# A two-layer decoder trunk with expert lookup: one 8 KB gather per token for u and v, and all V rows summed on TensorE

## What is computed

```python
def _peer(h, w_q, sub_keys, u_tab, v_tab):
    ...
    def chunk(xc):
        q = (xc @ w_q).reshape(C, PEER_HEADS, 2, PEER_HALF)
        s = jnp.einsum('thpd,hpkd->thpk', q, sub_keys).astype(jnp.float32)
        sv, si = lax.top_k(s, PEER_TOPK)
        ...
        top, pos = lax.top_k(cand, PEER_TOPK)
        eidx = jnp.take_along_axis(cidx, pos, axis=-1)
        g = jax.nn.softmax(top, axis=-1)
        a = jnp.einsum('thkd,td->thk', u_tab[eidx], xc).astype(jnp.float32)
        w = (g * jax.nn.gelu(a)).astype(xc.dtype)
        return jnp.einsum('thk,thkd->td', w, v_tab[eidx])
```

## Time and profile before

| | us |
|---|---|
| median of 3 runs (lowest, highest) | 3302.86 (3289.01, 3326.77) |
| the profiled execution, its own time | 3275.28 |
| its span, first to last instruction | 3273.5 |
| first dot of a gathered row | 147.7 |

### The profile page before, as it was taken

How to read it: one execution, slowest core, us unless ns; L and a number is a source line. 1 busy time by engine, 2 the same in 40 slices (tenths; PEclk the granted TensorE clock), 3 DMA queues, 4 the chain that set the end, 5 groups by cost and what they waited for, 6 DMA issues and landing times. The chain is left out here.

```text
span 3273.5 us, 27575 instructions
## 1 busy us (share of the span) xinstructions
PE 2517.0 (77%) x7696; PEld 1421.7 (43%) x7696; DVE 2320.6 (71%) x5442; ACT 677.6 (21%) x1655; POOL 2313.0 (71%) x2052
## 2 busy tenths in 40 slices
PE   6569877987778779977787887987688777666667
PEld 5446444753444435633444444643354443222222
DVE  2495779668789985668569887577667888555554
ACT  2112212123312211123112122133411211100000
POOL 0256767666777777777778777777777777777776
PEclk9779988988888889988898888998899899877888
DMA  6499999998999999999999999999999999999999
GB/s 262 159 333 414 383 411 401 359 393 310 345 411 379 377 358 411 411 410 366 373 410 388 377 390 357 412 381 344 348 394 410 362 382 365 369 368 381 367 371 350
DMA packets 317239, 1210.29 MB, mean 370 GB/s; under 512 B 37280, under 2 KB 37536, under 8 KB 301728
## 3 DMA queue, kind: packets, MB, share of 16 engines
q0 software_dynamic: 294912, 1073.87, 85.4%
q1 hardware_dynamic: 22176, 134.66, 10.3%
HBM read 1206.29 MB, written 2.10 MB: 369 GB/s over the span
## 5 line engine op out<-in xcount | busy, mean ns | idle before, releaser
L832 PE MATMUL psY<-ring,diag 128*128 128x512 f32 x3120 | 1642.2, 671 | 469.2 <-DMA ring<-in_v,idx 203.2
L482 POOL DMA_INDIRECT ring<-in_u,idx x1024 | 1155.1, 1128 | 573.1 <-issue 293.6
L1094 DVE CUSTOM_DVE_ANT_0 ring<-ring,htok 128x1024 f32<-128x1024 f32 x1024 | 1232.7, 1223 | 373.6 <-DMA ring<-in_u,idx 326.8
L482 POOL DMA_INDIRECT ring<-in_v,idx x1024 | 1157.7, 1131 | 375.5 <-issue 303.9
L832 PEld LDWEIGHTS psY<-ring,diag 128*128 128x128 f32 x3120 | 638.0, 214 | 1265.3 <-issue 897.7
L1103 DVE SCALAR_TENSOR_TENSOR x<-ring,wgt,x 128x1024 f32<-128x1024 f32 x244 | 313.6, 1285 | 40.9 <-DMA ring<-in_v,idx 35.1
L704 PE MATMUL psP<-hT,wr 128*128 128x256 f32 (+1 forms) x1664 | 328.9, 354 | 11.3 <-issue 10.1
L708 PE MATMUL psP<-wr,hT 128*128 128x256 f32 x1344 | 313.2, 387 | 15.9 <-issue 8.6
L704 PEld LDWEIGHTS psP<-hT,wr 128*128 128x128 f32 x1664 | 285.7, 202 | 82.1 <-issue 55.5
L708 PEld LDWEIGHTS psP<-wr,hT 128*128 128x128 f32 x1344 | 261.1, 195 | 89.1 <-issue 43.7
L671 ACT ACTIVATE diag<-cst,wgt 128x128 f32<-128x128 f32 x780 | 252.7, 390 | 132.9 <-DVE wgt L1114 67.2
(11 more groups left out here) (125 smaller groups left out, 1660.3 us busy)
## 6 DMA issues: line engine op xcount, KB each, us to landing
wr<-in_w_in SPq DMA_DIRECT2D x44, 1024.0 KB
wr<-in_w_q SPq DMA_DIRECT2D x40, 1024.0 KB
ring<-in_u,idx POOLq DMA_INDIRECT x1024
ring<-in_v,idx POOLq DMA_INDIRECT x1024
wr<-in_w_out SPq DMA_DIRECT2D x16, 1024.0 KB
ring<-in_w_in SPq DMA_DIRECT2D x11, 1024.0 KB, 17.0
probs<-in_subkeys SPq DMA_DIRECT2D x5, 1024.0 KB
ring<-in_w_out SPq DMA_DIRECT2D x4, 1024.0 KB, 15.2
```

Source lines behind the costliest of these rows:

```text
L482: pool.indirect_dma_start(out=ring[:, q % NB], out_offset=None, in_=table, in_offset=bass.IndirectOffsetOnAxis(ap=idx[:, s % NS, n:n + 1], ...
L832: last = nc.tensor.matmul(psY[:, b * 512:(b + 1) * 512], diag[:, m % ND], r[:, b * 512:(b + 1) * 512], start=first, stop=final)
L1094: v.tensor_tensor_reduce(out=r, in0=r, in1=htok[:, s % NS], scale=1.0, scalar=0.0, op0=ALU.mult, op1=ALU.add, accum_out=adot[:, J % 2, k:k ...
```

## The change

The two tables of a layer are joined into one of 8 KB rows (u, then v) when inputs are prepared. POOL issues one gather a row, 1024 in place of 2048, into a ring of `NR` = 10 slots of 8 KB per partition (80 KB in place of 76). The slot is free when the row's v part has been summed. The lag of a head goes: DVE takes the dot of row q, ACT then makes Gelu, weight and diagonal for that row alone (`NG` = 1 row at a time), and writes the diagonal over the first 128 numbers of the row's u part; PE sums row q - 3 (`ROW_LAG`) from the slot. `vector_rows` is empty, so PE sums all 1024 rows. The product with the gate moves from DVE (once a head) to ACT (once a row). The buffers `diag` and the semaphore `a_gelu` go. The schedule of the other parts is not touched. The early pieces lie in ten slots in place of nine.

```diff
-NB = 19
+NR = 10
...
-ND = 12
-LEAD = 5
+NG = 1
+ROW_LAG = 3
...
 def vector_rows(J):
-    return BUSY_ROWS.get(J, (3, 7, 11, 15))
...
+    return ()
...
-        ring = sb("ring", [P, NB, D])
+        ring = sb("ring", [P, NR, 2 * D])
...
         def _(pool):
-            for q, (kind, J, k) in enumerate(plan):
...
+            for q in range(SLOTS * STEPS):
+                J, k = divmod(q, TOPK)
+                s, n = divmod(q, SLOTS)
+                if k == 0:
+                    pool.wait_ge(idx_ready, TOP_NO[s, J % PH] + 1)
                     if J == 0:
                         pool.wait_ge(piece_ready, W_EARLY)
-                if q >= NB:
-                    k0, J0, i0 = plan[q - NB]
-                    if k0 == "u":
-                        pool.wait_ge(dotted, TOPK * J0 + i0 + 1)
-                    else:
-                        by, m = V_NO[J0, i0]
-                        pool.wait_ge(vx_used if by else v_used, m + 1)
...
+                if q >= NR:
+                    by, m = V_NO[divmod(q - NR, TOPK)]
+                    pool.wait_ge(vx_used if by else v_used, m + 1)
+                pool.indirect_dma_start(out=ring[:, q % NR], out_offset=None, in_=tables[s // NC],
...
         def _(act):
...
+            for q in range(SLOTS * STEPS + 1):
+                if q and q % NG == 0:
+                    J, k = divmod(q - NG, TOPK)
+                    s, n = divmod(q - NG, SLOTS)
+                    act.wait_ge(dotted, q)
+                    link(nc.scalar.activation(gl[:, J % 2, k:k + NG], adot[:, J % 2, k:k + NG], ACT.Gelu_apprx_tanh))
+                    if k == 0:
+                        act.wait_ge(gate_ready, TOP_NO[s, J % PH] + 1)
+                    for i in range(NG):
+                        last = nc.scalar.activation(wgt[:, J % 2, k + i:k + i + 1], gate[:, s % NS, n + i:n + i + 1], ACT.Copy,
+                                                    scale=gl[:, J % 2, k + i:k + i + 1])
+                    last.then_inc(w_ready, 1)
+                    act.wait_ge(w_ready, q // NG)
+                    for i in range(NG):
+                        if V_NO[J, k + i][0] == 0:
+                            nc.scalar.activation(ring[:, (q - NG + i) % NR, 0:P], ident, ACT.Copy,
+                                                 scale=wgt[:, J % 2, k + i:k + i + 1]).then_inc(diag_ready, 1)
+                for part, s, i in at_slot("act", q):
+                    front(s, part, i)
...
         def _(pe):
...
+            for q in range(SLOTS * STEPS + ROW_LAG):
+                r = q - ROW_LAG
+                by, m = V_NO.get(divmod(r, TOPK), (1, 0))
+                if by == 0:
...
+                    landed(pe, r)
+                    pe.wait_ge(diag_ready, m + 1)
...
+                    for b in range(2):
+                        last = nc.tensor.matmul(psY[:, b * 512:(b + 1) * 512], ring[:, r % NR, 0:P],
+                                                ring[:, r % NR, D + b * 512:D + (b + 1) * 512], start=first, stop=final)
+                    last.then_inc(v_used, 1)
```

More of the change, by code:

```diff
@@ L211, in constants @@
     return c
[L214 to L223, removed]
 def trunk(nc, x_in, cst_in, w_in, w_out, w_q, subkeys, w_sgu, b_sgu, conv_w, g_mix, g_head, g_ffn,
           g_sgu, g_qd, g_kd, g_qs, g_ks, *rest):
-    tables_u, tables_v, out = rest[:DEPTH], rest[DEPTH:2 * DEPTH], rest[2 * DEPTH]
-    plan = gather_plan()
-    at = {g: q for q, g in enumerate(plan)}
+    tables, out = rest[:DEPTH], rest[DEPTH]
     with ExitStack() as ctx:
@@ L319, in trunk @@
         w_landed = [sem(f"w_landed{i}") for i in range(NW)]
-        we_landed = [sem(f"we_landed{i}") for i in range(NB // 2)]
-        g_landed = [sem(f"g_landed{i}") for i in range(NB)]
+        we_landed = [sem(f"we_landed{i}") for i in range(NR)]
+        g_landed = [sem(f"g_landed{i}") for i in range(NR)]
         piece_ready = sem("piece_ready")
@@ L819, in _ @@
                     front(s, part, i)
[L820 to L836, removed]
+            for q in range(SLOTS * STEPS + ROW_LAG):
+                r = q - ROW_LAG
+                by, m = V_NO.get(divmod(r, TOPK), (1, 0))
+                if by == 0:
+                    s = r // SLOTS
+                    first, final = m == v_rows(PH * s, 0), m == v_rows(PH * (s + 1), 0) - 1
+                    landed(pe, r)
+                    pe.wait_ge(diag_ready, m + 1)
+                    if first and s:
+                        pe.wait_ge(x_done, s)
+                    for b in range(2):
+                        last = nc.tensor.matmul(psY[:, b * 512:(b + 1) * 512], ring[:, r % NR, 0:P],
+                                                ring[:, r % NR, D + b * 512:D + (b + 1) * 512], start=first, stop=final)
+                    last.then_inc(v_used, 1)
+                for part, s, i in at_slot("pe", q):
+                    front(s, part, i)
         @block.vector
@@ L1087, in _ @@
                     front(s, part, i)
[L1088 to L1102, removed]
-                        v.scalar_tensor_tensor(out=xs, in0=ring[:, at[("v", J - 1, k)] % NB],
-                                               scalar=wgt[:, (J - 1) % 2, k:k + 1], in1=xs,
-                                               op0=ALU.mult, op1=ALU.add).then_inc(vx_used, 1)
-                    for part, s1, i in at_slot("dve", J * TOPK + k):
-                        front(s1, part, i)
-                if J < HEADS:
-                    dve.wait_ge(gate_ready, TOP_NO[s, h] + 1)
-                    dve.wait_ge(a_gelu, J + 1)
-                    if J >= 2:
-                        dve.wait_ge(diag_ready, v_rows(J - 1, 0))
-                    v.tensor_tensor(wgt[:, J % 2], gl[:], gate[:, s % NS, h * TOPK:(h + 1) * TOPK], ALU.mult).then_inc(w_ready, 1)
-                if J >= PH and J % PH == 0:
-                    add_peer(J // PH - 1)
@@ new lines, in _ @@
+            for q in range(SLOTS * STEPS + VROW_LAG + 1):
+                if q < SLOTS * STEPS:
+                    J, k = divmod(q, TOPK)
+                    landed(dve, q)
+                    u = ring[:, q % NR, 0:D]
+                    v.tensor_tensor_reduce(out=u, in0=u, in1=htok[:, q // SLOTS % NS], scale=1.0, scalar=0.0,
+                                           op0=ALU.mult, op1=ALU.add, accum_out=adot[:, J % 2, k:k + 1]).then_inc(dotted, 1)
+                r = q - VROW_LAG
+                J, k = divmod(r, TOPK)
+                by, m = V_NO.get((J, k), (0, 0))
+                if by:
+                    xs = x[:, r // SLOTS % NC]
+                    landed(dve, r)
+                    dve.wait_ge(w_ready, r // NG + 1)
+                    if m:
+                        dve.wait_ge(vx_used, m)
+                    v.scalar_tensor_tensor(out=xs, in0=ring[:, r % NR, D:], scalar=wgt[:, J % 2, k:k + 1], in1=xs,
+                                           op0=ALU.mult, op1=ALU.add).then_inc(vx_used, 1)
+                if r >= SLOTS and r % SLOTS == 0:
+                    add_peer(r // SLOTS - 1)
+                for part, s, i in at_slot("dve", q):
+                    front(s, part, i)
```

51 lines of the change are left out of this document (10 added, 41 removed).

## The result

The median is 3114.9 us (3112.7 to 3116.7) against 3297.5 before in the same comparison: a ratio of 0.943, 95% interval 0.937 to 0.949. The forecast was 3183 with a range of 3060 to 3370. The profiled execution took 3113.4 us, its span 3111.5.

The account below looks back on a forecast made before the run. The prediction took GpSimd's issue rate as the bound, the DMA engines just beneath. Floor 3032 + 53 + 40 + 30 = 3155 us of span, 3157 with 1.8 around it, times 1.0084 = 3183 us; range 3060 to 3370.

Parts of the forecast that it names:

- GpSimd's issue rate is the bound: Kernel before: two gathers a row take GpSimd 2.84 us, against 2.55 us of the DMA engines, the bound just beneath.
- A gather of 8 KB costs what one of 4 KB does: GpSimd's gathers: 1.13 us plus 0.29 of issue each, bounds 0.93 and 2.3 us, so GpSimd leaves the path.
- Transfers at 411 GB/s: Whole run: the same 1182 MB take 2875 us; with start and end a floor of 3032 us.
- TensorE's load in the mixer of steps 2 and 3, +53: There TensorE's 370 us exceed 327 us of transfers: 43 us more, and 10 for handoffs.
- Later mixers +40, top-k +30: Weight pieces with TensorE's rows add 12, 20 and 8 for handoffs; VectorE's load near transfers adds 10 per top-k stage.
- ScalarE hidden: ScalarE's chain of about 1.1 us a row, with 281 table loads, is hidden by the ring and costs nothing on average.
- The ring: a cycle of 21 us: Each of ten slots is held 21 us, against 25.5 us at 2.55 us a row: four and a half to spare.
- Rival, TensorE at 592 ns: TensorE becomes the bound if V rows cost 592 ns a matmul everywhere: 3391 us, chance 0.09.
- Rival, lockstep: Waits on VectorE, ScalarE and TensorE in turn hold slots beside other work, 3.3 us a row: 3440 us, chance 0.14.
- Rival, no change: The dips belong to transfers or slots, not GpSimd; the rate stays 378 GB/s: about 3300 us, chance 0.14.
- The step to the median's terms: The profiled execution lay 0.8% under the median of runs, so 3157 us was scaled by 1.0084 to 3183.

Follow-up runs that it names:

- a_two_gathers: The changed kernel with its 8 KB gather split into two of 4 KB rows, one of u and one of v, into the same slot: 3376.9 us.
- a_no_gelu: The changed kernel with the rows' Gelu replaced by a copy, so 230 of 281 table loads go: 3084.2 us.
- a_vec_8_14: The changed kernel with 8 of 16 V rows of heads 8 to 14 back on VectorE, 56 rows: 3093.5 us.
- a_ring8: The changed kernel with eight ring slots in place of ten: 3158.3 us.
- a_lag1: The changed kernel with TensorE one row behind in place of three: 3423.7 us.

## Why the prediction was right

The direction and the mechanism held, and the time was 68 us better than forecast, inside the range.

- *GpSimd's issue rate is the bound.* Right for the kernel as a whole, and shown by a_two_gathers: one more gather a row gives back 262 us. The last stretch has it pure, at 2.84 us a row where the prediction had 2.84 (the last digit by luck, above); beside the mixers waits for slots came to it. In the mixer of steps 2 and 3 of the kernel before a gather was issued every 1.67 us and not every 1.42, so that stage was not at GpSimd's pace even then.
- *A gather of 8 KB costs what one of 4 KB does.* Right, 1.136 us, where the upper end would have left GpSimd on the path. That a dot stretches gathers was seen again (up to 2.0 us); GpSimd now stands 1717 us for slots, so it has the room.
- *Transfers at 411 GB/s.* Mis-sized. The trace of before has 4 KB rows only; 8 KB rows reach 421. For 1182 MB that would be 2808 us in place of 2875, a term too large by up to 67 us and the largest single miss; 20 of these could be had from the best 4 KB slice before (414). From the first dot to the last the bytes took 2954 us, so the stages lie 146 over the transfers at 421, where the prediction's additions were 53 + 40 + 30 = 123. The additions were thus too small in sum, and the good total rests in part on two misses of opposite sign.
- *TensorE's load in the mixer of steps 2 and 3, +53.* Right in place and sign; it came to 407 us against a sum of 380 (327 + 53). TensorE was busy 364 of the 370 foreseen and stood 43 where I gave 10. What the sum lacked is time in which TensorE stands, and a_no_gelu and a_vec_8_14 show that this part does not go with load: it fell by 11 us without the table loads at the same load, and rose from 43 to 83 with 57 us of load less. Table loads are thus a part of it; the rest is put down to handoffs, which no run isolates.
- *Later mixers +40, top-k +30.* The two later mixers and the three top-k stages came out shorter than the sum. The later mixers sum to 903 us, against 434 + 450 + 32 + 8 = 924 at 411 GB/s; the top-k stages to 833, against 254 + 285 + 291 + 30 = 860. Of those 48 us the higher rate explains up to 41 (1714 us of transfers, less 2.4%). Measured from transfers at 421 GB/s, the mixers stand 40 over and the top-k stages 23, so these two terms were about the right size.
- *ScalarE hidden.* Wrong by 31 us: the chain is 0.2 + 0.3 + 0.4 us, inside the bounds given, but its table loads are not hidden (a_no_gelu). The prediction called the ring thin there and costed it at nothing.
- *The ring: a cycle of 21 us.* The number is refuted as a minimum by a_ring8 (at most 20), and it was wrong in kind: landings come late because the queue is full, 20.2 us with ten slots and 15.3 with eight at the same 2.50 us a row. So the ring had more room than thought in the last stretch, and less in the top-k stages, where two slots fewer cost 27 us.
- *Rival, TensorE at 592 ns.* Refuted. In the last stretch a row's four matmuls took 1.96 us, 490 ns each, against the 570 from which the rival decides. The mean of 609 ns on the page counts time in which matmuls overlap; all 4096 together keep TensorE busy 1911 us, 467 ns each. The granted clock is 0.965 over the run, 0.98 in the last stretch, where it was 0.82 with a quarter of the rows on VectorE.
- *Rival, lockstep.* Not this kernel, but one number away from it (a_lag1, 3424 us).
- *Rival, no change.* Refuted: with the same bytes and fewer slots, but half the gathers, the last 166 rows went from 466 us to 413, and with the gathers doubled again in that same ring to 469.
- *The step to the median's terms.* I scaled by 1.0084, 26 us. The changed kernel's profiled execution lies at its median (3113.4, 3114.9), so this step accounts for about 26 of the 68 us. The rest lies in the span, foreseen at 3155 and measured at 3111.5.

That the V rows cost rather than gain had been worked out only as a load of TensorE. The runs put it at 61 us on the kernel before and about 19 on the changed one, where the three mixers lose 33 us and the other stages give part of it back.

## What to carry to other kernels

A DMA share of 96% does not say that transfers are the bound; compare the GB/s of stretches, and look at whether the engine that issues ever waits for room. Where it hardly ever did, in this kernel, fewer and larger gathers were worth 262 us, and nothing that was done to the engines that use the data was worth more than 39. And where several engines take turns on a row in program order, the lag between them is as important as the number of buffers: too short a lag cost 10% here, two buffers fewer of ten 1.4%.

## What the runs showed of the hardware

- GpSimd's time for an indirect gather of 128 rows is 1.13 us in the mean, whether the rows are 4 or 8 KB, with 0.30 us between two. Beside no VectorE instruction it is 0.93 to 0.95 us (240 gathers of the kernel before, 145 of the changed one); beside a dot it reaches 2.0.
- Gathers of 8 KB rows reached 421 GB/s over 80 us, of 4 KB rows 409 to 414 (windows of 26 to 82 us).
- ScalarE's product of two columns (128x1, a scale from memory) took 295 ns, more than the Gelu of one column, 198. The Trainium skill (ScalarE: Activation LUTs, What ACT_TABLE_LOAD costs) says that each operand read through a one-column pointer adds about 93 ns; the trace agrees, with 97.
- A table load takes 1.28 us, and working row by row brought two for each gate. Without the Gelu's there were 230 loads fewer, which brought 31 us.
